# Level products of ten triangular inverses, on the columns that each level renews

## The reference, cut to what matters

```
a_mat = beta[..., :, None] * jnp.einsum('nhcid,nhcjd->nhcij', k, k) * d_strict
rhs = jnp.concatenate([beta[..., None] * v, (beta * gam)[..., None] * k], axis=-1)
sol = lax.linalg.triangular_solve(a_mat, rhs, left_side=True, lower=True, unit_diagonal=True)
```

## Time and profile before

| | before |
|---|---|
| median of 3 runs | 2013.85 us (2013.14 to 2021.18) |
| the profiled execution's own time | 2016.32 us |
| its span, first to last instruction | 2014.5 us |
| TensorE matmuls busy | 1764.4 us |
| VectorE busy | 864.8 us |
| ScalarE busy | 592.6 us |
| mean granted TensorE clock | 0.966 |

### The profile page before, as it was taken

The page is one execution under the profiler, slowest core; times in us unless marked ns, Lnnn a source line. Parts: engine busy times, 40 slices in busy tenths (PEclk is TensorE's granted clock), DMA queues, the critical chain, the costliest instruction groups (busy, mean ns, idle before and its releaser), DMA issues.

```text
span 2014.5 us, 44025 instructions
## 1 busy us (share of the span) xinstructions
PE 1764.4 (88%) x17970; PEld 1034.2 (51%) x17970; DVE 864.8 (43%) x1514; ACT 592.6 (29%) x1018; POOL 246.9 (12%) x270
## 2 busy tenths in 40 slices
PE   5998995977877877998998889999999997899996
PEld 2444543544443443447765774454448755753452
DVE  1667433211111111558656753160467657542331
ACT  3414520000000000343315424261253334323442
POOL 0002211111111111006204000001011103000001
PEclk9999997999999999999999999999999999999998
DMA  9767035999999998421000012110211000012101
GB/s 356 257 229 257 1 116 197 398 423 424 426 424 423 423 425 364 184 73 34 3 3 2 3 49 79 42 43 32 79 43 35 3 2 2 3 65 103 42 1 42
DMA packets 75098, 307.75 MB, mean 153 GB/s; under 512 B 10908, under 2 KB 22300, under 8 KB 57888
## 3 DMA queue, kind: packets, MB, share of 16 engines
q1 hardware_dynamic: 63280, 291.98, 37.0%
q0 software_dynamic: 5360, 9.33, 1.3%
q10 hardware_dynamic: 6272, 3.81, 0.7%
HBM read 301.01 MB, written 16.52 MB: 158 GB/s over the span
## 4 chain that ended last, share of the span: by engine, by line
PE 72%; DVE 13%; another core or an unknown queue 5%; ACT 4%; issue 3%; DMA 2%; ACTq 1%; DVEq 0%; POOL 0%; SPq 0%; POOLq 0%
PE bank L495 13%; PE bank L2243 11%; PE bank L2259 6%; PE bank L1022 5%; PE bank L524 5%; PE bank L531 4%; PE bank L2081 3%; PE bank L2165 3%; PE bank L993 2%; DVE arena L1588 2%; DMA arena<-w_gate 2%; PE bank L2093 1%; PE bank L2105 1%; ACT arena L1034 1%
## 5 line engine op out<-in xcount | busy, mean ns | idle before, releaser
L495 PE MATMUL bank<-hT,arena 128*128 128x512 f32 (+1 forms) x640 | 288.8, 607 | 3.8 <-ACTq L1035 2.4
L2243 PE MATMUL bank<-arena 128*64 128x256 f32 x1792 | 214.2, 396 | 68.5 <-remote 66.1
L524 PE MATMUL bank<-arena 64*64 64x64 f32 x6656 | 214.4, 220 | 21.7 <-DVE arena L1716 7.4
L524 PEld LDWEIGHTS bank<-arena 64*64 64x64 f32 x6656 | 202.5, 135 | 36.3 <-DVE arena L1716 10.5
L2243 PEld LDWEIGHTS bank<-arena 128*64 128x64 f32 x1792 | 133.8, 142 | 158.9 <-issue 108.4
L495 PEld LDWEIGHTS bank<-hT,arena 128*128 128x128 f32 (+1 forms) x640 | 123.1, 194 | 162.3 <-issue 157.8
L2849 DVE COPY arena<-bank 128x256 f32<-128x256 f32 x32 | 13.6, 425 | 329.4 <-PE bank L2251 329.4
L2259 PE MATMUL bank<-arena 128*64 128x512 f32 x448 | 104.0, 606 | 16.4 <-remote 16.4
L1022 PE MATMUL bank<-arena 128*128 128x512 f32 x256 | 110.4, 593 | 0.0
L1034 ACT ACTIVATE arena<-bank 128x512 f32<-128x512 f32 (+2 forms) x124 | 73.2, 590 | 120.8 <-PE bank L495 80.9
L531 PE MATMUL bank<-hT,arena 128*128 128x512 f32 x224 | 106.1, 612 | 0.0
(11 more groups left out here) (448 smaller groups left out, 2692.7 us busy)
## 6 DMA issues: line engine op xcount, KB each, us to landing
arena<-w_gate SPq DMA_DIRECT2D x28, 2048.0 KB, 30.7
arena<-w_up SPq DMA_DIRECT2D x28, 2048.0 KB, 20.9
arena<-w_down SPq DMA_DIRECT2D x28, 2048.0 KB, 26.1
arena<-w_ada SPq DMA_DIRECT2D x12, 2048.0 KB, 18.2
arena<-w_in SPq DMA_DIRECT2D x10, 2048.0 KB, 11.5
arena<-w_out SPq DMA_DIRECT2D x6, 2048.0 KB, 7.7
arena<-w_in SPq DMA_DIRECT2D x6, 1536.0 KB, 6.5
hT<-w_up SPq DMA_DIRECT2D x4, 2048.0 KB, 20.9
```

Source lines behind the costliest of these rows:

```text
L495: m = pe.matmul(bank[b][0:w, :], slot2(n)[:, k, c:c + w], hT[:, k, :], start=(k == 0), stop=(k == KD - 1))
L524: m = pe.matmul(o[half(f), s, t], lhs[half(f), s, t], rhs[half(f), s, t], start=True, stop=True)
L2243: mm = pe.matmul(bank[b][c * CAP:(c + 1) * CAP, 0:FE // 2], XT[j][:, k % 4, k // 4, :], e_slot(e_at(e, i), KD)[:, k, c * (FE // 2):(c + 1) ...
```

## The change

All operations between levels are cut to the columns that the level renews. `fresh` takes from a view of 64n columns the runs of z = 2^l of one parity: the lower or the upper half of each group of 2z, by direction and by which triangle is filled. The streamed operand and the output of each level product, the ScalarE copy of V, and the predicated copies with their masks go through it: 32 of 64 columns in a matmul (runs of 2, 4, 8, 16, 32), 256 of 512 elements in the others. The weights of each matmul (the left operand), the transposes, all counts, the order and the semaphores are as before.

```
+        def fresh(ap, d, l, upper):
+            odd = int(upper == (d == 0))
+            return ap.rearrange("p (g w z) -> p g w z", w=2, z=1 << l)[:, :, odd, :]
+        def fresh8(ap, d, l, upper):
+            return fresh(ap, d, l, upper).rearrange("p (a g) z -> p a g z", a=2 * TT)
+        def merged_fresh(d, l, upper):
+            a = C2["up" if upper == (d == 0) else "low"][0] + l * CG
+            m = fresh(c2[:, a:a + CG].bitcast(U32), d, l, upper)
+            return m.rearrange("p (a g) z -> p a g z", a=1).to_broadcast([P, 2 * TT, CG >> (l + 1), 1 << l])
...
-                        m = pe.matmul(o[half(f), s, t], lhs[half(f), s, t], rhs[half(f), s, t], start=True, stop=True)
+                        m = pe.matmul(cols(o[half(f), s, t]), lhs[half(f), s, t], cols(rhs[half(f), s, t]), start=True, stop=True)
...
+                        cols = [[lambda m, d=d, l=l, upper=upper: fresh(m, d, l, upper) for upper in (False, True)] for d in range(2)]
...
-                            product(d, g_Bn[d], g_T[d]).then_inc(sem(f"g_v_done{d}"), 1)
+                            product(d, g_Bn[d], g_T[d], cols[d][0]).then_inc(sem(f"g_v_done{d}"), 1)
...
-                                product(2 + d, g_Y[d], g_V[d]).then_inc(sem(f"g_t_done{d}"), 1)
+                                product(2 + d, g_Y[d], g_V[d], cols[d][0]).then_inc(sem(f"g_t_done{d}"), 1)
                             else:
-                                product(2 + d, g_V[d], g_Y[d]).then_inc(sem(f"g_t_done{d}"), 1)
+                                product(2 + d, g_V[d], g_Y[d], cols[d][1]).then_inc(sem(f"g_t_done{d}"), 1)
...
-                            act.activation(g_V[d], bank[d], ACT.Copy).then_inc(sem(f"g_v_full{d}"), 1)
+                            act.activation(fresh(g_V[d], d, l, False), fresh(bank[d], d, l, False), ACT.Copy).then_inc(sem(f"g_v_full{d}"), 1)
...
-                                dve.copy_predicated(blocks(g_T[d]), merged(d, l, False), blocks(bank[2 + d])).then_inc(sem(f"g_t_full{d}"), 1)
+                                dve.copy_predicated(fresh8(g_T[d], d, l, False), merged_fresh(d, l, False), fresh8(bank[2 + d], d, l, False)).then_inc(sem(f"g_t_full{d}"), 1)
```

More of the change, by code:

```diff
@@ L518, in pe_second, with product @@
             pairs_in = [(t, f) for t in range(TT) for f in range(2)]
-            def product(b, lhs, rhs):
+            def product(b, lhs, rhs, cols=lambda m: m):
                 o, lhs, rhs = pieces(bank[b]), pieces(lhs), pieces(rhs)
@@ L725, in rwkv_chunks @@
                     for l in range(1, LEVELS):
+                        cols = [[lambda m, d=d, l=l, upper=upper: fresh(m, d, l, upper) for upper in (False, True)] for d in range(2)]
                         for d in range(2):
                             t_full[d].wait()
-                            product(d, r_Bn[d], r_bt[:, ct, d]).then_inc(sem(f"g_v_done{d}"), 1)
+                            product(d, r_Bn[d], r_bt[:, ct, d], cols[d][0]).then_inc(sem(f"g_v_done{d}"), 1)
                         for d in range(2):
@@ L733, in rwkv_chunks @@
                             if l < LEVELS - 1:
-                                product(2 + d, Y, V).then_inc(sem(f"g_t_done{d}"), 1)
+                                product(2 + d, Y, V, cols[d][0]).then_inc(sem(f"g_t_done{d}"), 1)
                             else:
-                                product(2 + d, V, Y).then_inc(sem(f"g_t_done{d}"), 1)
+                                product(2 + d, V, Y, cols[d][1]).then_inc(sem(f"g_t_done{d}"), 1)
                     if ct == 1:
@@ L1257, in act_second @@
                             v_done[d].wait()
-                            act.activation(r_kr[:, ct, d, 0], bank[d], ACT.Copy).then_inc(sem(f"g_v_full{d}"), 1)
+                            act.activation(fresh(r_kr[:, ct, d, 0], d, l, False), fresh(bank[d], d, l, False), ACT.Copy).then_inc(sem(f"g_v_full{d}"), 1)
                         if ct == 0 and l in (2, 3):
@@ L1592, in dve_second @@
                             else:
-                                dve.copy_predicated(blocks(g_Y[d]), merged(d, l, True), blocks(bank[2 + d])).then_inc(sem(f"g_y_full{d}"), 1)
+                                dve.copy_predicated(fresh8(g_Y[d], d, l, True), merged_fresh(d, l, True), fresh8(bank[2 + d], d, l, True)).then_inc(sem(f"g_y_full{d}"), 1)
                         if l in (2, 3):
@@ L1715, in dve_second @@
                             if l < LEVELS - 1:
-                                dve.copy_predicated(blocks(Tm), merged(d, l, False), blocks(bank[2 + d])).then_inc(sem(f"g_t_full{d}"), 1)
+                                dve.copy_predicated(fresh8(Tm, d, l, False), merged_fresh(d, l, False), fresh8(bank[2 + d], d, l, False)).then_inc(sem(f"g_t_full{d}"), 1)
                                 n_t[d] += 1
@@ L1720, in dve_second @@
                             else:
-                                dve.copy_predicated(blocks(Y), merged(d, l, True), blocks(bank[2 + d])).then_inc(sem(f"g_y_full{d}"), 1)
+                                dve.copy_predicated(fresh8(Y, d, l, True), merged_fresh(d, l, True), fresh8(bank[2 + d], d, l, True)).then_inc(sem(f"g_y_full{d}"), 1)
                         if ct == 0 and l in (1, 2):
```

## The result

The changed kernel took 2050.6 us in the median (2029.0 to 2060.8, 4 runs), the kernel before 2016.2 (2013.1 to 2021.2, 4 runs): a ratio of 1.013, 95% interval 1.010 to 1.017. The ratio compares the means without the run of 2060.8 us, which counts as slow because it is over 1.5% above the fastest; with it the ratio is 1.015. The changed kernel is slower, outside the range of 1984 to 2014, and on the side to which 0.07 was given. The profiled execution took 2056.0 us, with a span of 2054.2, 39.7 more than before, and a mean granted clock of 0.929 instead of 0.966. The four executions of the changed kernel line up by this clock: 2029.0 us at 0.943, 2045.2 at 0.935, 2056.0 at 0.929, 2060.8 at 0.924.

What follows compares the result with a forecast made beforehand. TensorE's products (3.87 us a level) and the 4.27 us chain through VectorE were taken as limits; gaining mostly 0.40 us a level, 20.5 us in two layers, gave 1993.4 us from 2013.85, range 1984 to 2014.

Steps and rivals of the forecast that it cites:

- the side to which 0.07 was given: Whole kernel: the outcome that the change makes it slower, chance 0.07.
- rival D: Stages: TensorE's clock falls to 1.2 GHz as it streams half as much; 3.9 us more a level; chance 0.03.
- the product's term: Level products: records stay 30.2 ns apart with 32 columns, set by weight loads; four products take 3.87 us a level.
- TensorE's floor thus stays at 3.87 us: Each level: four products, 128 records at 30.2 ns, take 3.87 us, unchanged by the cut.
- Products at full clock: Level products: record spacing unchanged at 30.2 ns, because weights stay 64 columns wide; range 28.5 and 15.1.
- Strides in the products: Level products streaming strided runs, two elements at level 1 to 32 at level 5: no cost taken.
- Predicated copies: VectorE, each level: 0.717 to 0.46 us for 256 elements, 0.53 less a level for the pair.
- Rival B: VectorE: strided operations cost as whole rows did, leaving only ScalarE's 1.3 us at level 1: 2012.6 us; chance 0.11.
- ScalarE copies: Copies of V: 0.597 to 0.383 us, mostly hidden; at level 1 of ht stages 0.21 gained, three times a layer.
- The sum without the clock: Ten stages: gains add to 10.2 us a layer, 20.5 us in two layers.
- so the gain reaches the end: Behind the stages: TensorE's queue runs on, so the 20.5 us come off the whole span.
- Rival A: Level products: the stream sets their time and they halve to 0.48 us each; 1954 us; chance 0.10.

Runs made afterwards that it cites:

- e1: Changed kernel with level products streaming all 64 columns again, ScalarE and predicated copies still cut: 2001.6 us, ratio 0.992 to the kernel before.
- e10: Kernel of e1 run once more, whole products with cut elementwise operations: 2001.1 us, ratio 0.991 to the kernel before.

## Why the prediction was wrong

**The step that failed** is rival D, and with it the product's term. "TensorE's granted clock falls to 1.2 GHz in the stages, because it streams half as much" got 0.03, and is what happened. The argument against it was one window of 2 us with TensorE mostly idle at clock 1.00. That row shows one short pause at full clock; it says nothing of a stretch of matmuls that each stream half as long, for 20 us, and no row of before had such a stretch, as the same sentence admitted. The price was right in kind: 3.9 us more a level was given for half clock, 6.83 - 3.74 = 3.1 was measured, since records went from 29.2 to 53.3 ns and not from 30.2 to 60; 18 periods of the 40 between first and last predicated copies ran so, and 18 x 3.1 = 56 us is about the whole distance to the version with whole products. What was wrong is the chance, and the sentence "TensorE's floor thus stays at 3.87 us": it holds at one of two clocks.

What the runs show of the cause: 32 columns streamed in all ten stages, strided or dense, with cut or whole elementwise operations, lost the clock in some stages of each profile, and their other executions have mean clocks of 0.924 to 0.943; 64 columns, strided or dense, in none of the profiled ones; 48 on average, in one stage for a short time. Of the changed kernel, the executions with a lower mean clock were the longer ones. By its records TensorE was as busy in the stages as before or busier. The Trainium skill ("TensorE: Matmul & The Clock Gate", section "What's actually happening") has the clock depend on how busy the engine has been. In records' time this trace speaks against it: 33.28 of 33.46 us were busy at 0.51. What goes with the fall in these runs are records that stream 32 columns behind 64 weight columns; why that is so no run shows. Open is also why one stage falls and the same stage in the other layer doesn't, why ht=1 and ht=2 kept the clock when they alone were cut, and why the products with both sides at 32 mostly kept the clock.

**Products at full clock**: right. 29.2 ns a record with 32 columns, 29.3 with 64; the weight load holds it, as the runs with 32 weight columns show.

**Strides in the products**: right, nothing (the strided 64 columns).

**Predicated copies**: 0.46 was taken, 0.43 for d=0 and 0.39 for d=1 measured from level 2 on at full clock. At level 1, with runs of two elements, the row is 0.73 and 0.69 for 256 elements, no less than for 512 before. Rival B was thus right for that level: its period in ht=1 is 4.24 against 4.29. That is a fifth of these copies, and 0.4 us a stage.

**ScalarE copies**: 0.386 measured, 0.383 taken; level 1 too.

**The sum without the clock**: whole products gained 13.2 us from span to span and 16.7 by the ratio, where 20.5 were forecast. In the stages the sum fits: the ten windows of before add up to 235.8 us, those of e1 to 215.2, 20.6 less. Between first and last predicated copies, ct=1 gave 1.62 us a stage (1.60 forecast), ht=1 1.78 (1.82), ct=0 1.69 (2.15). Level 1 gave nothing (its share in ct=0 was part of the 2.15), and the others a little more than assumed, since 29.3 ns a record and not 30.2 hold once nothing interrupts the run. In ht=0 the period that VectorE fills was counted for both layers, but the second layer has none: its four periods of before are 17.37 us and not 17.88. What didn't hold is "so the gain reaches the end": from the first predicated copy of the first stage to the end of the span 17.6 us were gained (17.4 in e10), some 3 less than in the stages. The rest of the gap to 13.2 lies ahead of the first stage, where e1's execution was 4.4 us late.

**Rival A** fell: in the levels' products with 64 weight columns and 32 streamed, records stayed 29.2 ns apart.

## What to carry to other kernels

Cutting the streamed columns of a small matmul below the width of its weights bought nothing here, for the weight load sets the distance of records (29.2 ns with 32 columns streamed, 29.3 with 64). Cutting both sides brought it to 16.1 ns, but the one kernel that did so and still computes every level, at level 5 alone, was no faster as a whole. The narrower stream can cost the clock: here it took a stage from 21 to 33 us while TensorE's records left next to no idle time, so busy time alone doesn't show it. Look at the granted clock of each stretch and at the distance of records. Before a forecast leans on a price per level, price it at both clocks, and ask of any edit that makes TensorE's work thinner whether the trace has one stretch as thin, as long, at full clock.

## What was not expected of the hardware

- The granted clock went to 0.50 and stayed there for up to 33 us with matmuls back to back (records 53.3 ns apart, 32 columns each). After the change, in all five stages that fell, it came back only 1 to 4 us behind the stage, with other matmuls.
- A predicated copy of 256 elements in runs of two takes 0.68 to 0.73 us, in runs of four and more 0.39 to 0.45; a ScalarE copy of the same elements out of PSUM takes 0.38 at either.
- Matmuls with 32 weight columns and 32 streamed start 16.1 ns apart in a short run, but between long ones TensorE stopped for 0.25 to 1.5 us with no releaser in the trace.
